# Attention with each query scaled and rotated two heads ahead

## The chip, the cores and the metric

The kernel runs on one core of a Trainium2 chip. The metric is the device time of one execution in microseconds (us), as the median of several. A core has engines with queues of their own, which wait for one another through semaphores: TensorE (PE, matmuls and transposes), VectorE (DVE), ScalarE (ACT), GpSimd (POOL) and SyncE (SP, which issues the DMAs).

## What is computed

The program is two layers of a model on 512 tokens of width 1024: a layer with gated linear attention and an MLP, and a hybrid layer that adds a gated delta rule and a sparse attention, with another MLP. The change touches the sparse attention of the second layer. For each of 8 query heads (2 key heads, 4 query heads to each, head size 128):

```
a_q = apply_partial_rope(rms_norm_2(a_q.reshape(B, S, ATT_HEADS, ATT_HEAD_DIM), q_norm_g), cos, sin)
...
s = jnp.einsum('bqcgd,bqncd->bqcgn', qg, k_g).astype(jnp.float32) * scale
s = jnp.where(valid[:, :, None, None, :], s, -jnp.inf)
p = jax.nn.softmax(s, axis=-1).astype(v_g.dtype)
o = jnp.einsum('bqcgn,bqncd->bqcgd', p, v_g)
```

The keys that a query may see (`valid`) are chosen once for all heads by an indexer, ahead of this stage. `apply_partial_rope` rotates the first 32 of the 128 dimensions by an angle that depends on the token.

## The kernel before

The kernel runs stage by stage, with a fence between the larger ones. The stage here is `pe_att`, `act_att`, `dve_att` and `pool_att`, one function for each engine. It stands behind the input projections and the choice of keys, and ahead of the delta rule (`pe_gdn` and so on). All operands lie in SBUF. The queries of all heads are in `q_all`, the reciprocal root mean squares of them in `q_sq`.

The loop `att_steps` goes through the heads in an order in which key head `e` alternates: step i = 2j + e. Two steps stand in the body of a loop over j that runs three times, and the last two are written out behind it. The scores of all 512 queries against the keys are made in four causal blocks of 512, 256, 128 and 384 keys (`S_ORDER`). Work of a step, with the lines of before:

- **scaling** of a query (`queries`, L1421, VectorE): query by gain by reciprocal root mean square, into `aq[:, e]`. It signals `r_y`.
- **rotation**: a matmul with the swap matrix on TensorE (`pe_rope`, L1112, in two passes), at the same time the product with the cosines on GpSimd (`pool_rope`, L1117), then two ops on VectorE (`dve_rope`): product of the matmul's result with the sines (L1123), and the sum (L1126), which signals `rp_out`.
- **scores** (L1374, TensorE): four matmuls, each in two passes (x8 in the rows). VectorE adds the mask as it takes them out of PSUM (L1436), takes the row maxima (L1440) and scales them (L1444).
- **softmax**: exponentials and row sums on ScalarE (L1408), reciprocals (L1452) and scaling of the probabilities (L1456) on VectorE.
- **transposes** of the probabilities (L1388, ten on TensorE), their copies out of PSUM on ScalarE (L1413), and the **product with the values** (L1395, four matmuls in eight passes).
- **output** (`output`, L1429, VectorE): result by gate, into `o_att`.

There are two buffers `aq` and `ms` (scores and probabilities), one for each e, and one PSUM bank for the rotation matmul. In step i of before, VectorE scales and rotates the query of head i+1 first, then normalizes head i, masks head i+1 and ends with the output of head i. TensorE rotates and scores head i+1 first, then transposes and multiplies head i. The engines' orders are fixed by this text; there is no scheduler.

Of the kernel before, what the change touches and what calls it, by code (L numbers as in the profile page):

```python
# [101 lines left out]
def build(nc, t, out, const_square, const_wide, gb_rows):  # L102
    with ExitStack() as ctx:
# [37 lines left out]
        def take(*shape):  # L141

            n = int(np.prod(shape))
            v = arena[:, at[0]:at[0] + n]
            at[0] += n
            assert at[0] <= 22400, at[0]
            if len(shape) == 2:
                v = v.rearrange("p (a b) -> p a b", a=shape[0])
            if len(shape) == 3:
                v = v.rearrange("p (a b c) -> p a b c", a=shape[0], b=shape[1])  # L150
            return v
# [883 lines left out]
        ca, sa = take(SEQ), take(SEQ)  # L1035
# [9 lines left out]
        aq = take(2, SEQ)  # L1045
# [62 lines left out]
        def pe_rope(pe, c, src, swap):  # L1108

            if not (isinstance(c, int) and c == 0):  # L1110
                pe.wait_ge(s["rp_ss"], c)
            pe.matmul(b[5][:], swap[:], src, start=True, stop=True).then_inc(s["rp_ps"], 1)  # L1112
# [6 lines left out]
        def dve_rope(dve, c, src, sin):  # L1119
            if not (isinstance(c, int) and c == 0):  # L1120
                dve.wait_ge(s["rp_out"], c)
            dve.wait_ge(s["rp_ps"], c + 1)
            dve.tensor_tensor(rp_s, b[5][:], sin, ALU.mult).then_inc(s["rp_ss"], 1)  # L1123
            dve.wait_ge(s["rp_cc"], c + 1)
            dve.wait_ge(s["rp_ss"], c + 1)
            dve.tensor_tensor(src, rp_c, rp_s, ALU.add).then_inc(s["rp_out"], 1)  # L1126
# [225 lines left out]
        HPK = ATT_H // ATT_KV  # L1352
# [5 lines left out]
        def att_steps(eng, body):  # L1358

            with eng.Fori(0, HPK - 1) as j:  # L1360
                body(j, 0, True)
                body(j, 1, True)
            body(HPK - 1, 0, True)
            body(HPK - 1, 1, False)

        def pe_att(pe):
            def front(i, e):

                pe.wait_ge(s["r_y"], i + 3)
                pe_rope(pe, i + 7, aq[:, e], swap_a)  # L1370
                pe.wait_ge(s["rp_out"], i + 8)
                for q in S_ORDER:
                    bk, o = s_at[q]
                    last = pe.matmul(bk[:, o:o + P * (q + 1)], aq[:, e, q * P:(q + 1) * P], ak[:, e, 0:P * (q + 1)],  # L1374
                                     start=True, stop=True)
                    if q != 0:
                        last.then_inc(s["s_ps"], 1)

            def body(j, e, more):
                i = 2 * j + e  # L1380
                if more:
                    pe.wait_ge(s["ms_r"], TT * i + TT)
                    front(i + 1, 1 - e)
                pe.wait_ge(s["pn_r"], TT * i + TT)
                for k in K_ORDER:
                    bk, o = t_at[k]
                    for q in range(k, TT):
                        last = pe.transpose(bk[:, o + (q - k) * P:o + (q - k + 1) * P],  # L1388
                                            ms[e][:, off[q] + k * P:off[q] + (k + 1) * P], ident[:])
                    if k != 3:  # L1390
                        last.then_inc(s["pt_ps"], 1)
                pe.wait_ge(s["att_done"], i + 1)
                for n, k in enumerate(K_ORDER):
                    pe.wait_ge(s["pt_sb"], TT * i + n + 1)
                    last = pe.matmul(b[4][:, k * P:SEQ], v_key[e][:, k, :], p_t[:, koff[k]:koff[k] + SEQ - k * P],  # L1395
                                     start=(n == 0), stop=(n == TT - 1), skip_group_check=True)
                last.then_inc(s["pv_ps"], 1)

            front(0, 0)
            att_steps(pe, body)  # L1400

        def act_att(act):
            def body(j, e, more):
                i = 2 * j + e
                act.wait_ge(s["nms"], i + 1)
                for q in S_ORDER:
                    m = ms[e][:, off[q]:off[q] + P * (q + 1)]
                    act.activation(m, m, ACT.Exp, scale=P ** -0.5, bias=n_max[:, 4 * e + q:4 * e + q + 1],  # L1408
                                   accum_out=r_sum[:, q:q + 1]).then_inc(s["ex_a"], 1)
                for n, k in enumerate(K_ORDER):  # L1410
                    act.wait_ge(s["pt_ps"], (TT - 1) * i + (1, 2, 3, 3)[n])
                    bk, o = t_at[k]
                    act.copy(p_t[:, koff[k]:koff[k] + SEQ - k * P], bk[:, o:o + SEQ - k * P]).then_inc(s["pt_sb"], 1)  # L1413

            att_steps(act, body)

        def dve_att(dve):
            def queries(j, e):
                i, h = 2 * j + e, j + HPK * e
                dve.wait_ge(s["r_r"], h + 3)  # L1420
                dve.scalar_tensor_tensor(aq[:, e], q_all[:, bass.ds(h, 1)].rearrange("p a t -> p (a t)"),  # L1421
                                         gains[:, G_QN:G_QN + 1], q_sq[:, bass.ds(h, 1)].rearrange("p a t -> p (a t)"),
                                         ALU.mult, ALU.mult).then_inc(s["r_y"], 1)

            def output(j, e):
                i, h = 2 * j + e, j + HPK * e
                dve.wait_ge(s["pv_ps"], i + 1)
                o = o_att[:, bass.ds(h, 1)].rearrange("p a t -> p (a t)")
                dve.scalar_tensor_tensor(o, o, 1.0, b[4][:], ALU.add, ALU.mult).then_inc(s["att_done"], 1)  # L1429

            def scores(i, e):
                for n, q in enumerate(S_ORDER):
                    dve.wait_ge(s["s_ps"], (TT - 1) * i + (1, 2, 3, 3)[n])
                    w = P * (q + 1)
                    bk, o = s_at[q]
                    dve.scalar_tensor_tensor(ms[e][:, off[q]:off[q] + w], sel[:, off[q]:off[q] + w], BIG, bk[:, o:o + w],  # L1436
                                             ALU.mult, ALU.add).then_inc(s["ms_r"], 1)
                for n, q in enumerate(S_ORDER):
                    dve.wait_ge(s["ms_r"], TT * i + n + 1)
                    dve.tensor_reduce(n_max[:, 4 * e + q:4 * e + q + 1], ms[e][:, off[q]:off[q] + P * (q + 1)], AX.X, ALU.max,  # L1440
                                      negate=True).then_inc(s["nm_r"], 1)
                dve.wait_ge(s["nm_r"], TT * i + TT)
                nm = n_max[:, 4 * e:4 * e + 4]
                dve.tensor_scalar(nm, nm, P ** -0.5, None, ALU.mult).then_inc(s["nms"], 1)  # L1444

            def body(j, e, more):
                i = 2 * j + e
                if more:
                    queries(j + e, 1 - e)
                    dve_rope(dve, i + 8, aq[:, 1 - e], sa)  # L1450
                dve.wait_ge(s["ex_a"], TT * i + TT)
                dve.reciprocal(r_sum, r_sum).then_inc(s["rs_r"], 1)  # L1452
                dve.wait_ge(s["rs_r"], i + 1)
                for q in S_ORDER:
                    m = ms[e][:, off[q]:off[q] + P * (q + 1)]
                    dve.tensor_scalar(m, m, r_sum[:, q:q + 1], None, ALU.mult).then_inc(s["pn_r"], 1)  # L1456
                if more:
                    scores(i + 1, 1 - e)
                output(j, e)

            queries(0, 0)
            dve_rope(dve, 7, aq[:, 0], sa)
            scores(0, 0)
            att_steps(dve, body)

        def pool_att(pool):
# [684 lines left out]
        @block.tensor  # L2151
        def _(pe):
            pe_start(pe)
            pe_norm(pe)
            pe.wait_ge(s["memsets"], 3)
            fence(pe, 1)
            pe_gates(pe)
            pe_gla(pe)
            pe.wait_ge(s["gla_done"], GLA_H + 1)
            fence(pe, 2)  # L2160
            pe_wout(pe, N_WO0, 0, 2 * (GLA_H - 1))
            pe_mlp(pe, N_FF0, 0, KT)
            fence(pe, 3)
            pe_two_norms(pe)
            pe_in1(pe)
            pe_att(pe)
            fence(pe, 4)
            pe_gdn(pe)
            pe.wait_ge(s["gdn_done"], GDN_H + 1)
            fence(pe, 5)  # L2170
            pe_wout(pe, N_WO1, 1, GDN_H - 1)
            pe_mlp(pe, N_FF1, 1, 3 * KT)
            pe_out(pe, KT - 1)
# [83 lines left out]
```

## Time and profile before

| | us |
|---|---|
| median of 3 runs | 1844.41 (1842.42 to 1846.32) |
| profiled execution | 1836.11 |
| its span, from first to last record | 1834.5 |
| TensorE busy | 1693.3 (92%) |
| VectorE busy | 1014.1 (55%) |
| ScalarE busy | 715.4 (39%) |
| GpSimd busy | 247.9 (14%) |

All times in rows below are those of the profiled execution, counted from the start of its span. A row of the chain of waits is a piece of the path that ended last: when it began, how long it held the path, and which engine and line it was. The attention stage lies in it from 882.6 to 976.4 us.

### The profile page before, as it was taken

How to read it: one execution, taken by the hardware profiler on the slowest of the kernel's cores; microseconds unless marked ns; L12 is line 12 of the kernel's file. 1: busy time of each engine (PE TensorE's matmuls, PEld its weight loads, DVE VectorE, ACT ScalarE, POOL GpSimd, SP SyncE). 2: the span in 40 equal slices, each digit the busy share in tenths (PEclk: the TensorE clock that was granted, in tenths of full speed). 3: DMA queues.
4: the chain of work that ended last, by engine and by line, in shares of the span. 5: the costliest groups of instructions: out<-in, count | busy, mean ns of one | idle time of the engine just before them, and what ended most of it. 6: DMA issues, size and time to landing. Idle time of an engine off the chain costs nothing.

```text
span 1834.5 us, 25379 instructions
## 1 busy us (share of the span) xinstructions
PE 1693.3 (92%) x9258; PEld 1327.9 (72%) x9258; DVE 1014.1 (55%) x1511; ACT 715.4 (39%) x1106; POOL 247.9 (14%) x216
## 2 busy tenths in 40 slices
PE   6899968999999978899668999999998899999999
PEld 3788856888888855567336777777776678888887
DVE  5455545444454455478676566766575544444443
ACT  6344433323132334224434455555454342323232
POOL 0134440000000030234110222211122000000000
PEclk8999979999999998999899999999999999999999
DMA  4222202233333332223002222222121233333333
GB/s 133 69 59 69 70 12 81 81 104 91 103 92 93 101 99 58 56 68 85 23 0 58 70 54 63 58 63 62 50 58 36 60 89 99 96 93 97 96 95 101
DMA packets 258153, 135.01 MB, mean 74 GB/s; under 512 B 10700, under 2 KB 254941, under 8 KB 258069
## 3 DMA queue, kind: packets, MB, share of 16 engines
q1 hardware_dynamic: 258068, 133.84, 26.2%
q8 instruction: 59, 0.97, 0.2%
q14 instruction: 26, 0.21, 0.0%
HBM read 131.64 MB, written 2.18 MB: 73 GB/s over the span
## 4 chain that ended last, share of the span: by engine, by line
PE 69%; DVE 12%; issue 10%; POOL 4%; ACT 3%; DVEq 1%; DMA 0%; POOLq 0%; ACTq 0%; PEldq 0%; SPq 0%; PEld 0%
PE bank L231 15%; PE bank L233 15%; PE bank L232 15%; PE bank L1616 4%; PE bank L490 4%; PE bank L492 3%; PE bank L491 3%; DVE arena L1316 1%; POOL arena L781 1%; PE bank L1374 1%; POOL arena L798 1%; PE bank L1112 1%; PE bank L1395 1%; DVE arena L1312 1%; DVE w_lo L215 1%
## 5 line engine op out<-in xcount | busy, mean ns | idle before, releaser
L215 DVE TENSOR_TENSOR w_lo<-raw,w_hi 128x1024 fp32r<-128x1024 f32 x218 | 280.9, 1289 | 103.8 <-ACT w_hi L211 100.8
L211 ACT CAST w_hi<-raw 128x1024 fp32r<-128x1024 f32 x234 | 245.0, 1047 | 229.2 <-PE bank L233 213.1
L231 PE MATMUL bank<-h_hi,w_hi 128*128 128x512 f32 x760 | 306.1, 403 | 24.7 <-DVE h_lo L993 10.2
L232 PE MATMUL bank<-h_lo,w_hi 128*128 128x512 f32 x760 | 298.8, 393 | 0.0
L233 PE MATMUL bank<-h_hi,w_lo 128*128 128x512 f32 x760 | 298.8, 393 | 0.0
L231 PE MATMUL bank<-m_hi,w_hi 128*128 128x512 f32 x608 | 239.2, 393 | 6.9 <-DVE w_lo L215 6.7
L233 PE MATMUL bank<-m_hi,w_lo 128*128 128x512 f32 x608 | 238.1, 392 | 0.0
L232 PE MATMUL bank<-m_lo,w_hi 128*128 128x512 f32 x608 | 237.8, 391 | 0.0
L490 PE MATMUL bank<-h_hi,w_hi 128*128 128x512 f32 x472 | 211.6, 448 | 0.0
L231 PEld LDWEIGHTS bank<-h_hi,w_hi 128*128 128x128 f32 x760 | 144.6, 190 | 70.7 <-issue 20.2
L492 PE MATMUL bank<-h_hi,w_lo 128*128 128x512 f32 x472 | 186.3, 395 | 0.0
L491 PE MATMUL bank<-h_lo,w_hi 128*128 128x512 f32 x472 | 185.8, 394 | 0.0
L232 PEld LDWEIGHTS bank<-h_lo,w_hi 128*128 128x128 f32 x760 | 144.9, 191 | 31.4 <-issue 2.5
L233 PEld LDWEIGHTS bank<-h_hi,w_lo 128*128 128x128 f32 x760 | 144.4, 190 | 30.7
L231 PEld LDWEIGHTS bank<-m_hi,w_hi 128*128 128x128 f32 x608 | 115.0, 189 | 34.1 <-issue 7.3
L233 PEld LDWEIGHTS bank<-m_hi,w_lo 128*128 128x128 f32 x608 | 114.8, 189 | 24.2
L232 PEld LDWEIGHTS bank<-m_lo,w_hi 128*128 128x128 f32 x608 | 114.9, 189 | 23.6
L929 DVE TENSOR_TENSOR arena<-bank,arena 128x512 f32<-128x512 f32 x64 | 44.3, 692 | 147.0 <-PE bank L233 147.0
L919 DVE TENSOR_TENSOR arena<-arena 128x512 f32<-128x512 f32 x64 | 44.3, 692 | 133.2 <-ACT arena L895 133.2
L490 PEld LDWEIGHTS bank<-h_hi,w_hi 128*128 128x128 f32 x472 | 89.5, 190 | 29.7 <-issue 13.1
L895 ACT ACTIVATE arena<-bank 128x512 f32<-128x512 f32 x64 | 38.5, 601 | 175.3 <-PE bank L233 175.3
L1616 PEld LDWEIGHTS bank<-arena 64*64 64x64 f32 x1984 | 74.6, 139 | 43.2 <-issue 35.8
(275 smaller groups left out, 2285.5 us busy)
## 6 DMA issues: line engine op xcount, KB each, us to landing
raw<-in_l_w_ff SPq DMA_DIRECT2D x64, 512.0 KB, 4.0
raw<-in_w_in SPq DMA_DIRECT2D x64, 512.0 KB, 3.8
raw<-in_w_mlp_up SPq DMA_DIRECT2D x32, 512.0 KB, 4.0
raw<-in_w_mlp_down SPq DMA_DIRECT2D x32, 512.0 KB, 3.9
raw<-in_l_w_in SPq DMA_DIRECT2D x24, 512.0 KB, 3.8
raw<-in_l_w_out SPq DMA_DIRECT2D x8, 512.0 KB, 3.7
arena<-gb_rows SPq DMA_DIRECT2D x16, 256.0 KB, 3.9
raw<-in_w_out SPq DMA_DIRECT2D x8, 512.0 KB, 3.8
```

The costliest lines, as they stand in the source:

```text
L211: act.copy(w_hi[q.par][:], raw[q.par][:]).then_inc(s["w_hi_ready"], 1)
L215: dve.tensor_tensor(w_lo[q.par][:], raw[q.par][:], w_hi[q.par][:].bitcast(F32), ALU.subtract).then_inc(s["w_ready"], 1)
L231: pe.matmul(g_bank[q.par][:], w_hi[q.par][:, k], hi[:, k], start=(k == 0), stop=False)
L232: pe.matmul(g_bank[q.par][:], w_hi[q.par][:, k], lo[:, k], start=False, stop=False)
L233: last = pe.matmul(g_bank[q.par][:], w_lo[q.par][:, k], hi[:, k], start=False, stop=(k == KT - 1))
L490: pe.matmul(g_bank[q.par][:], w_hi[q.par][:, k], hi[:, k], start=(k == 0), stop=False)
L491: pe.matmul(g_bank[q.par][:], w_hi[q.par][:, k], lo[:, k], start=False, stop=False)
L492: last = pe.matmul(g_bank[q.par][:], w_lo[q.par][:, k], hi[:, k], start=False, stop=(k == KT - 1))
L895: act.activation(rl[:, u % 2], g_bank[q.par][:], ACT.Relu).then_inc(s["rl"], 1)
L919: dve.tensor_tensor(sq[:, u % 2], rl[:, u % 2], rl[:, u % 2], ALU.mult).then_inc(s["sqr"], 1)
L929: dve.tensor_tensor(down[:, u % 2], g_bank[q.par][:], r_sqr, ALU.mult).then_inc(s["dn"], 1)
L1616: return pe.matmul(o, left, right, start=True, stop=True, skip_group_check=True)
```

## The change

The scaling and rotation of a query move from one head ahead to two heads ahead. The boolean `more` becomes a number `ahead` (2 in the loop, 1 and 0 in the last two steps). TensorE's `front` is split: the rotation matmul (`turn`) of head i+2 is issued behind the product with the values of head i, and the scores (`scores`) of head i+1 stay at the start of the step. On VectorE the scaling of head i+2 is issued behind the row maxima of head i+1, ahead of the output of head i, and the rotation's two ops behind that output. Ahead of the loop, head 1 is scaled and rotated beside the scores of head 0. ScalarE's and GpSimd's orders are as before.

```diff
             with eng.Fori(0, HPK - 1) as j:
-                body(j, 0, True)
-                body(j, 1, True)
-            body(HPK - 1, 0, True)
-            body(HPK - 1, 1, False)
+                body(j, 0, 2)
+                body(j, 1, 2)
+            body(HPK - 1, 0, 1)
+            body(HPK - 1, 1, 0)
 
         def pe_att(pe):
-            def front(i, e):
+            def turn(i, e):
 
                 pe.wait_ge(s["r_y"], i + 3)
                 pe_rope(pe, i + 7, aq[:, e], swap_a)
+
+            def scores(i, e):
                 pe.wait_ge(s["rp_out"], i + 8)
...
-                if more:
+                if ahead >= 1:
                     pe.wait_ge(s["ms_r"], TT * i + TT)
-                    front(i + 1, 1 - e)
+                    scores(i + 1, 1 - e)
                 pe.wait_ge(s["pn_r"], TT * i + TT)
...
                 last.then_inc(s["pv_ps"], 1)
-
-            front(0, 0)
+                if ahead >= 2:
+                    turn(i + 2, e)
+
+            turn(0, 0)
+            scores(0, 0)
+            turn(1, 1)
             att_steps(pe, body)
...
-            def body(j, e, more):
+            def body(j, e, ahead):
                 i = 2 * j + e
-                if more:
-                    queries(j + e, 1 - e)
-                    dve_rope(dve, i + 8, aq[:, 1 - e], sa)
                 dve.wait_ge(s["ex_a"], TT * i + TT)
...
-                if more:
+                if ahead >= 1:
                     scores(i + 1, 1 - e)
+                if ahead >= 2:
+                    queries(j + 1, e)
                 output(j, e)
+                if ahead >= 2:
+                    dve_rope(dve, i + 9, aq[:, e], sa)
 
             queries(0, 0)
             dve_rope(dve, 7, aq[:, 0], sa)
+            queries(0, 1)
             scores(0, 0)
+            dve_rope(dve, 8, aq[:, 1], sa)
             att_steps(dve, body)
```

On TensorE, the first step of the loop before. L1112 is the rotation matmul of the next head, L1374 its scores, L1388 the transposes and L1395 the product with the values of the head in hand:

```order
L1369 REGISTER_ALU
L1111 REGISTER_ALU
L1112 MATMUL bank<-arena,swap_a 128x512
L1371 REGISTER_ALU
L1374 MATMUL bank<-arena 128x512
L1374 MATMUL bank<-arena 128x256
L1374 MATMUL bank<-arena 128x128
L1374 MATMUL bank<-arena 128x384
L1388 MATMUL bank<-ident,arena 128x128 x10
```

The same step after the change, where the scores are L1376, the transposes L1390 and the product with the values L1397:

```order
L1376 MATMUL bank<-arena 128x384
L1390 MATMUL bank<-ident,arena 128x128 x10
L1394 REGISTER_ALU
L1396 REGISTER_ALU
L1397 MATMUL bank<-arena 128x512
L1396 REGISTER_ALU
L1397 MATMUL bank<-arena 128x256
L1396 REGISTER_ALU
L1397 MATMUL bank<-arena 128x128
L1397 MATMUL bank<-arena 128x384
L1369 REGISTER_ALU
L1112 MATMUL bank<-arena,swap_a 128x512
```

The rotation matmul has moved from the place directly ahead of the scores of its own head to behind the product with the values of the head two before it.

On VectorE, from the end of one step to the reciprocal of the next, before: L1444 ends the maxima, L1429 is the output, L1421 the scaling, L1123 and L1126 the rotation.

```order
L1444 TENSOR_SCALAR arena<-arena 128x4
L1429 ISA
L1429 SCALAR_TENSOR_TENSOR arena<-arena,bank 128x512
L1421 ISA
L1421 SCALAR_TENSOR_TENSOR arena<-q_all,gains,q_sq 128x512
L1122 REGISTER_ALU
```

After the change the maxima end with L1450, the scaling is L1427, the output L1435 and the reciprocal L1455:

```order
L1450 TENSOR_SCALAR arena<-arena 128x4
L1426 REGISTER_ALU
L1427 ISA
L1427 SCALAR_TENSOR_TENSOR arena<-q_all,gains,q_sq 128x512
L1435 ISA
L1435 SCALAR_TENSOR_TENSOR arena<-arena,bank 128x512
L1121 REGISTER_ALU
L1122 REGISTER_ALU
L1123 TENSOR_TENSOR arena<-bank,arena 128x512
L1126 TENSOR_TENSOR arena<-arena 128x512
L1455 RECIPROCAL arena<-arena 128x4
```

Scaling and output have changed places; the two ops of the rotation follow the output as before.

## Rows read from the trace of the kernel before

**Rows 1.** The page, its first line.

```profile
span 1834.5 us, 25379 instructions
```

**Rows 2.** Chain of waits, one head in mid-loop: start us, us, engine and line.

```profile
910.28 2.43 PE bank L1374 x8
912.71 1.09 PE bank L1388 x10
...
913.82 2.44 PE bank L1395 x8
...
916.40 0.06 DVE arena L1429
...
917.05 0.71 DVE arena L1421
...
917.88 1.14 PE bank L1112 x2
919.04 0.70 DVE arena L1123
...
919.84 0.70 DVE arena L1126
...
920.59 2.43 PE bank L1374 x8
```

**Rows 3.** Chain of waits, start of the stage.

```profile
886.22 4.65 PE bank L1374 x8
...
893.26 0.05 DVE arena L1444
...
893.60 0.76 DVE arena L1421
...
894.48 2.08 PE bank L1112 x2
...
898.13 4.33 PE bank L1374 x8
```

**Rows 4.** Timeline of VectorE: start, us, engine, line, op, out<-in, idle time before.

```profile
920.45 0.17 DVE L1452 RECIPROCAL arena<-arena 128x4 f32<-128x4 f32 x1
920.65 1.27 DVE L1456 TENSOR_SCALAR arena<-arena 128x512 f32<-128x512 f32 x4
921.84 1.01 DVE L1436 SCALAR_TENSOR_TENSOR arena<-arena,bank 128x512 f32<-128x512 f32 x2
...
923.72 1.66 DVE L1440 TENSOR_REDUCE arena<-arena 128x1 f32<-128x512 f32 x4
925.41 0.17 DVE L1444 TENSOR_SCALAR arena<-arena 128x4 f32<-128x4 f32 x1
```

**Rows 5.** Timeline of GpSimd in the same head as rows 2.

```profile
917.91 1.26 POOL L1117 TENSOR_TENSOR arena<-arena 128x512 f32<-128x512 f32 x1 [8.97 <-DVE arena L1421]
```

**Rows 6.** Chain of waits, last head to the next stage (L231).

```profile
961.71 2.44 PE bank L1374 x8
...
966.53 0.18 DVE arena L1444
...
966.74 2.30 ACT arena L1408 x8
...
970.60 2.39 PE bank L1388 x10
...
976.40 0.50 PE bank L231
```

**Rows 7.** Stretches: us, busy PE, PEld, DVE, ACT, POOL, granted clock, DMA share, GB/s.

```profile
898.00:902.00 4.00, 3.87 (x8) 2.36 (x9) 2.55 (x8) 0.00 (x0) 0.00 (x0) 0.50 0.00 0
902.00:904.00 2.00, 1.97 (x13) 1.43 (x12) 1.50 (x4) 1.06 (x4) 0.00 (x0) 0.99 0.00 0
910.00:920.00 10.00, 7.06 (x28) 4.01 (x28) 7.21 (x19) 3.70 (x12) 1.26 (x1) 1.00 0.00 0
971.00:973.00 2.00, 2.00 (x11) 2.00 (x10) 0.00 (x0) 0.86 (x2) 0.00 (x0) 0.50 0.00 0
```

More of the change, by code:

```diff
@@ L1397, in body @@
                 last.then_inc(s["pv_ps"], 1)
-            front(0, 0)
+                if ahead >= 2:
[3 more added lines that the diff above has]
+            turn(1, 1)
             att_steps(pe, body)
         def act_att(act):
-            def body(j, e, more):
+            def body(j, e, ahead):
                 i = 2 * j + e
@@ L1444, in scores, with body @@
                 dve.tensor_scalar(nm, nm, P ** -0.5, None, ALU.mult).then_inc(s["nms"], 1)
-            def body(j, e, more):
+            def body(j, e, ahead):
                 i = 2 * j + e
-                if more:
-                    queries(j + e, 1 - e)
-                    dve_rope(dve, i + 8, aq[:, 1 - e], sa)
                 dve.wait_ge(s["ex_a"], TT * i + TT)
```

## The prediction

> **What bounds the kernel now.** I read the page first, for the span [rows 1], and then the chain of waits through the attention stage, since only that stage is touched. The profiled execution took 1836.11 us around a span of 1834.5 us, so 1.6 us lie outside the span. The chain for one head in the middle of the loop [rows 2] is the base of everything below. TensorE computes the scores of the next head (2.43 us from 910.28), the ten transposes of the head in hand (1.09) and its product with the values (2.44), which ends at 916.26. Then nobody but VectorE has work: the output op (L1429) starts at 916.40, the scaling of the next query (L1421) at 917.05, TensorE rotates it from 917.88 (1.14), VectorE finishes the rotation with L1123 (919.04) and L1126 (919.84), and the next scores start at 920.59. So of each round 5.98 us are TensorE's big products, 1.62 us are output and scaling ahead of the rotation, and 2.71 us are the rotation itself. From 910.28 to the scores of the last head at 961.71 [rows 6] there are five rounds, (961.71 − 910.28) / 5 = 10.29 us each.
>
> Two other stretches differ. At the start [rows 3] the scores of head 0 take 4.65 us, the maxima end with L1444 at 893.26, and only then is head 1 scaled (893.60), rotated (894.48, 2.08 us) and multiplied (898.13). The matmuls there take about twice their later time (4.33 against 2.43, 2.08 against 1.14) because the granted clock was 0.50 in 898 to 902 (the 1.2 GHz level); it was 0.99 in 902 to 904 and 1.00 after [rows 7]. The round from 898.13 to 910.28 is thus 12.15 us. At the end [rows 6] nothing overlaps the last head, and from the scores at 961.71 to the next stage at 976.40 are 14.69 us.
>
> **The change, part by part.** I call the heads 0 to 7 in the order of the loop. Scaling and rotation of head i+2 now stand behind the row maxima of head i+1 and around the output of head i. Nothing is added or removed in count: eight scalings, eight rotations, and no DMA.
>
> *Middle rounds.* I lay VectorE out from the start of L1126 (919.84 is zero). As before [rows 4], the reciprocal starts at 0.61, the scaling of the probabilities at 0.81, masking at 2.00, the maxima at 3.88, and the small L1444 at 5.57. Now the scaling of the next query follows. The gap from L1444 to L1421 is 0.34 us at the start, with a loop branch in it [rows 3]; I take 0.30, so it runs from 5.87 to 6.62 (0.75 us). In the rows of before the rotation matmul starts 0.12 us behind the end of that op (917.76 to 917.88), so it could start at 6.74. TensorE itself has scores from 0.75 and the product with the values until 0.75 + 5.98 = 6.73. The two arrive together, which is the tight place of this change. Rotation at 6.75, L1123 at 6.75 + 1.16 = 7.91 (917.88 to 919.04), L1126 at + 0.80 = 8.71: that is the new round. The output op starts 0.14 us behind the product (6.87) and ends at 7.56, in the shadow of the rotation matmul; if that shadow were gone it would cost its 0.69 us. GpSimd's product (L1117, 1.26 us, 0.15 us behind the scaling [rows 5]) runs from 6.77 to 8.03, and L1126 needs it at 8.71. The exponentials (2.30 us [rows 6]) start 0.21 us behind L1444, end at 8.1, and the reciprocal wants them at 8.71 + 0.61. So a round goes from 10.29 to 8.71, saving 1.58; five of them save **7.9 us**. Bounds: if TensorE runs from one product into the next without a gap and VectorE's gap is 0.2, the round is 8.6 (saves 8.4); if the gap between L1444 and the scaling is twice the 0.34 of the row, it is 9.1 (saves 6.0).
>
> *Start.* The rotation matmul of head 1 follows the scores of head 0 directly (890.87, done at 892.95 even at 2.08 us). VectorE takes its result after L1444, a 0.17 us op [rows 4]: L1123 at about 893.26 + 0.21 = 893.47, L1126 at 894.27, scores of head 1 at 895.02 instead of 898.13. Saves **3.1 us**.
>
> *First round.* It was 12.15. Here the exponentials of head 0 are late: they can't start before 893.47 and end at 895.77, where in a middle round they are long done, so the reciprocal is at 895.8 and not at 894.9. If the clock is high, VectorE is the limit: scaling 896.0, masks 897.2, maxima 898.9, L1444 at 900.6, query scaled by 901.6, next scores 901.7 + 2.71 = 904.4, a round of 9.4. If it stays at 0.50 for the scores, as it did before, TensorE is: 4.33 + 3.55 + 0.05 + 2.71 = 10.65. I can't tell which, because TensorE now works without a break from 886.22 to near 892.9 but then waits about 2 us. I take 10.0: saves **2.1 us** (1.5 to 2.75).
>
> *End.* The last two heads keep their order; from the scores of head 7 to the next stage stays 14.69. In it the clock was at 0.50 in 971 to 973 [rows 7], and the transposes took 2.39 instead of 1.09. **0**, with 1.45 us to gain if that drop falls away. The branch of TensorE's loop now lies between a rotation and the scores behind it, under the 1.5 us of L1123 and L1126: 0.
>
> Sum: 3.1 + 2.1 + 7.9 = 13.1 us. Of the profiled 1836.11 us that leaves 1823.0. The median of the three runs shown is 8.3 us above the profiled execution, so I take the difference off it: 1844.41 − 13.1 = **1831.3 us**.
>
> **A rule weighed.** In the new order GpSimd's product lies beside the output op and L1123; before, it lay in an empty stretch of VectorE but for its very end. In the row it ran from 917.91 to 919.17, L1123 began at 919.04 inside it, and took its usual 0.70 [rows 2, 5]. The overlap is 0.13 us, too short to be proof. The Trainium skill, "SBUF — State Buffer", section "Who interferes with whom", says that a VectorE instruction with two SBUF inputs contends with a GpSimd instruction that reads SBUF, one fully blocking the other, and that one with at most one SBUF input does not. By that rule the output op and L1123, each with one operand from a PSUM bank, are free, and L1126, with two operands in SBUF, starts after the product. The sum would be the same 13.1 us; a reader who knows only that two engines share a port would subtract the 4.9 us of the second case below.
>
> **The rivals.**
> (1) *Forecast*, gain 11 to 15 us: chance 0.75.
> (2) *VectorE or GpSimd is late next.* If the output op had to wait for GpSimd's product (to 8.03), it would end at 8.72, L1126 would be at 9.52, and a round loses 0.81 us; six rounds lose 4.9. A gap of 0.7 us more ahead of the scaling would do the same. Gain 8.2: 1836.2 us. For it speaks that the query arrives within 0.1 us of when TensorE wants it; against it the L1123 row. Chance 0.10.
> (3) *The clock gives more.* TensorE was busy 7.06 of 10 us in 910 to 920 [rows 7] and would be busy 7.1 of 8.7. If the first round runs fast (0.6) and the drop at the end is gone (1.45), the gain is 15.2, 1829.2 us. If the runs behind the median, longer than the profiled one, had lost the clock for one head more, which the new order avoids, 6.3 us come on top (price below), 1823. Chance 0.09.
> (4) *It does nothing*: the rotation is still released by something behind the output, so that scaling and output merely swap. The round stays near 10.3 and only a part of the start is won. The order of instructions speaks against it. Within 0.2% of before: chance 0.02.
> (5) *Slower, by the clock.* The clock rose only after TensorE had worked unbroken from 898.13 to about 902. The new start breaks its work at 893 to 895, and if the level then stays at 1.2 GHz, each head costs 1.90 more for scores (4.33 against 2.43), 1.30 for transposes (2.39 against 1.09), 0.94 for the rotation and about 2.2 for the product with the values (an estimate: the same doubling, no row of it at that level): 6.3 us. From 13.1 / 6.3 = 2.1 heads on it decides; with four heads it is 12 us slower, 1856 us. Against it: every head now has 7 us of unbroken TensorE work, longer than the stretch that raised the clock. Chance 0.04.
>
> **How the numbers follow.** 0.2% is 3.7 us, about what a measurement of this kernel can tell from no change. (1), (2) and (3) are faster: 0.94. (4) is within: 0.02. (5) is slower: 0.04. The range runs from 1826, between the two figures of (3), to 1838, which is (2) with the 2 us by which the three runs lie about their median.
>
> **What would show it.** In the profile after: the scores of head 1 start about 8.8 us behind those of head 0 (11.9 before); rounds of 8.7 us between scores; the first one between 9.4 and 10.7; from the first scores to the next stage 77 us instead of 90.2; TensorE's idle time ahead of the rotation matmul nearly gone; the output op at its 0.69 us beside GpSimd's 1.27. I am wrong if the rotation matmul waits for the scaling for over 0.3 us in the middle rounds, if L1123 waits for the output op, or if the granted clock is 0.50 in any round but the first.

## The result, and the profile after

| | us |
|---|---|
| median before (4 runs) | 1844.59 (1842.42 to 1846.32) |
| median of the change (4 runs) | 1822.97 (1821.78 to 1824.64) |
| ratio of the runs | 0.9887, 95% interval 0.9873 to 0.9902 |
| profiled execution of the change | 1821.78, its span 1820.2 |

The change is faster by 21.6 us; the prediction was 13.1. The two profiled executions differ by 14.3 us in time and in span. So the profile moved about as forecast, and the median by half as much again as the profile.

The chain of waits of the changed kernel, at the start, in one head of mid-loop and at the end (scores are L1376 now, transposes L1390, product with the values L1397, the small op behind the maxima L1450):

```profile
span 1820.2 us, 25383 instructions
```

```profile
885.35 4.65 PE bank L1376 x8
...
892.38 0.04 DVE arena L1450
...
892.46 0.70 DVE arena L1123
...
894.00 4.11 PE bank L1376 x8
...
904.28 2.43 PE bank L1376 x8
...
912.86 2.43 PE bank L1376 x8
915.28 1.09 PE bank L1390 x10
...
916.40 2.43 PE bank L1397 x8
918.82 1.06 PE bank L1112 x2
...
919.91 0.70 DVE arena L1123
...
920.70 0.70 DVE arena L1126
...
921.45 2.43 PE bank L1376 x8
...
947.30 2.41 PE bank L1376 x8
...
956.16 2.39 PE bank L1390 x10
...
961.92 0.50 PE bank L231
```

Against [rows 2]: output and scaling are gone from the chain, and the rotation matmul follows the product with the values in the same instant (918.82). A middle round is 921.45 − 912.86 = 8.59 us, five of them (947.30 − 904.28) / 5 = 8.60; it was 10.29. Against [rows 3]: from the scores of head 0 to those of head 1 it is 8.65 us (11.91 before), and the first round is 10.28 (12.15). Against [rows 6]: the end is 14.62 (14.69). The stage, first scores to next stage, takes 76.6 us instead of 90.2. The last 0.7 of the 14.3 us had been gained ahead of it: the first scores start 0.87 us earlier than in the other execution, with nothing changed there.

VectorE and GpSimd in the timeline of the same head (start, us, engine, line, op, idle before):

```profile
917.68 0.17 DVE L1450 TENSOR_SCALAR arena<-arena 128x4 f32<-128x4 f32 x1
917.94 0.75 DVE L1427 SCALAR_TENSOR_TENSOR arena<-q_all,gains,q_sq 128x512 f32 x1
...
918.85 1.28 POOL L1117 TENSOR_TENSOR arena<-arena 128x512 f32<-128x512 f32 x1 [7.31 <-DVE arena L1427]
918.99 0.69 DVE L1435 SCALAR_TENSOR_TENSOR arena<-arena,bank 128x512 f32 x1 [0.30 <-PE bank L1397]
...
919.91 0.69 DVE L1123 TENSOR_TENSOR arena<-bank,arena 128x512 f32<-128x512 f32 x1 [0.23 <-PE bank L1112]
```

The scaling starts 0.26 us behind L1450 (0.30 was taken) and is done at 918.69, 0.13 us ahead of the 918.82 at which the chain turns to the rotation matmul. The margin is no larger than that: the load of the rotation's weights starts at 918.74, and the trace names the scaling as what released it. The output op keeps its 0.69 us beside GpSimd's 1.28 us, and L1123 waits for the matmul, not for the output.

### The profile page after: what moved, and what is told of

It reads as the page before. It is cut to its first block, busy times and chain, and to the rows that moved or that the text cites. A ratio compares the mean times of both kernels' runs of the same rounds, so it can differ in the third digit from the quotient of the medians.

```text
span 1820.2 us, 25383 instructions
## 1 busy us (share of the span) xinstructions
PE 1691.0 (93%) x9258; PEld 1328.1 (73%) x9258; DVE 1014.0 (56%) x1511; ACT 715.5 (39%) x1106; POOL 249.8 (14%) x216
## 4 chain that ended last, share of the span: by engine, by line
PE 69%; DVE 12%; issue 10%; POOL 4%; ACT 3%; DVEq 1%; DMA 0%; SPq 0%; POOLq 0%; ACTq 0%; PEldq 0%
PE bank L231 15%; PE bank L233 15%; PE bank L232 15%; PE bank L1625 4%; PE bank L490 4%; PE bank L492 3%; PE bank L491 3%; DVE arena L1316 1%; POOL arena L781 1%; PE bank L1376 1%; POOL arena L798 1%; DVE w_lo L215 1%; PE bank L1397 1%; DVE arena L1312 1%; PE bank L1112 1%
## 5 line engine op out<-in xcount | busy, mean ns | idle before, releaser
L231 PE MATMUL bank<-h_hi,w_hi 128*128 128x512 f32 x760 | 306.2, 403 | 25.1 <-DVE h_lo L993 10.2
L231 PE MATMUL bank<-m_hi,w_hi 128*128 128x512 f32 x608 | 239.2, 393 | 6.9 <-DVE w_lo L215 6.6
L231 PEld LDWEIGHTS bank<-h_hi,w_hi 128*128 128x128 f32 x760 | 144.5, 190 | 70.3 <-issue 19.7
L231 PEld LDWEIGHTS bank<-m_hi,w_hi 128*128 128x128 f32 x608 | 114.9, 189 | 34.2 <-issue 7.3
L490 PEld LDWEIGHTS bank<-h_hi,w_hi 128*128 128x128 f32 x472 | 89.5, 190 | 29.7 <-issue 13.1
```

Source lines behind the costliest of these rows:

```text
L231: pe.matmul(g_bank[q.par][:], w_hi[q.par][:, k], hi[:, k], start=(k == 0), stop=False)
L490: pe.matmul(g_bank[q.par][:], w_hi[q.par][:, k], hi[:, k], start=(k == 0), stop=False)
```

## The experiments

The question is where 7.3 us come from that no term of the sum has. The profiled execution of before was 8.3 us below the median that the prediction had (8.5 below that of the four runs), that of the change 1.2 us below its own. "This" below is the median of the kernel of the experiment, "before" that of the kernel before on the same chip.

### The kernel before, profiled once more

No edit.

> The kernel before, unchanged, profiled once more. The timed gain (21.6 us) is 7.3 us above what the two profiled executions differ by (14.3 us in both time and span), because the profiled execution of before was 8.3 us under the median. Clock theory: in most executions of before some rounds of the attention stage run partly at the low clock, since TensorE waits in two pieces of 1.6 us in each round; the stage from the first scores to the next stage is then about 97 to 99 us instead of 90.2, at 1840 to 1846 us in all, with granted clock below 1.00 in the middle rounds. Rival: the 8 us lie outside the stage (another chip, transfers); the stage is then 90.2 us again and some other stretch is longer.

Measured: the profiled execution took 1845.78 us, with these scores and last lines in the chain of waits:

```profile
888.98 4.65 PE bank L1374 x8
...
900.89 4.40 PE bank L1374 x8
...
913.10 4.63 PE bank L1374 x8
...
926.02 4.63 PE bank L1374 x8
...
939.02 4.11 PE bank L1374 x8
...
951.02 2.43 PE bank L1374 x8
...
971.58 2.44 PE bank L1374 x8
...
986.19 0.50 PE bank L231
```

and in its stretches (us, busy PE, PEld, DVE, ACT, POOL, granted clock, DMA share, GB/s):

```profile
910.00:913.00 3.00, 1.12 (x2) 0.30 (x2) 1.68 (x4) 0.18 (x2) 1.26 (x1) 0.79 0.00 0
913.00:917.00 4.00, 3.90 (x8) 2.39 (x9) 2.51 (x8) 0.00 (x0) 0.00 (x0) 0.50 0.00 0
...
948.00:958.00 10.00, 7.06 (x28) 4.01 (x28) 7.20 (x19) 3.39 (x12) 1.26 (x1) 1.00 0.00 0
```

In [rows 7] the first round was the only one at the low level. Here the clock falls in the middle rounds too. In 910 to 911 it is still 1.00, while the rotation matmul runs; in 912 to 913, in the wait behind it, it is 0.50 (0.79 over 910 to 913), and the scores that follow run at 1.2 GHz (0.50 in 913 to 917). The scores are slow in four rounds (those from 900.89, 913.10, 926.02 and 939.02), which take 12.2, 12.9, 13.0 and 12.0 us. The last two are 10.2 and 10.3, as in the first profile. The six rounds take 70.7 us against 63.6, and the stage 97.2 against 90.2: 7.0 of the 9.7 us between the two executions of one and the same kernel. The other 2.7 lie ahead of the stage, in work that is the same in all kernels here: the first scores start at 886.22 in the one profile and at 888.98 in the other. This profile is of one of the slowest of its ten executions, whose median is 1840.53 us.

What the others did is an estimate. In the ten profiles without extra matmuls ahead of the stage the first scores start between 885.35 and 889.74 us, and in all fourteen the rest behind the stage takes 856.8 to 859.9 us. With the 1.6 us outside the span, a stage of 90.2 us would give at most 889.7 + 90.2 + 859.9 + 1.6 = 1841.4 us. All four runs behind the median of 1844.59 are above that, and so are more than half of the 46 executions below.

Over 46 executions of the kernel before in all comparisons, the time went from 1834.72 to 1849.41 us and the mean granted clock of an execution from 0.967 to 0.956; their correlation is −0.95. This shows that time and clock go together, not in which stage. As a measure of such ratios: this run against before gave a ratio of 0.9981 (0.9962 to 0.9999) for two identical kernels, which is what a spread of 15 us does to a few runs.

### TensorE kept at work in the two waits, in the kernel before

```diff
-            def front(i, e):
+            def front(i, e, more=True):
+                if more:
+                    pe.matmul(b[0][:], ones[:], ca, start=True, stop=True)
                 pe.wait_ge(s["r_y"], i + 3)
                 pe_rope(pe, i + 7, aq[:, e], swap_a)
+                if more:
+                    pe.matmul(b[0][:], ones[:], ca, start=True, stop=True)
                 pe.wait_ge(s["rp_out"], i + 8)
...
-            front(0, 0)
+            front(0, 0, False)
```

> Before, with two matmuls of no use in each round of attention (ones by the cosine table into a scores bank that has been read), one in each of TensorE's two waits: ahead of the rotation matmul and behind it. Each lasts about 1.0 us and the waits 1.62 and 1.55 us, so in a run that keeps its clock they change nothing. Clock theory: median 6 to 9 us below before (1836 to 1838 us), granted clock 1.00 in every round but the first. Rival (the time lies elsewhere): the same as before within 2 us, or slower by what the fillers push in the slow first round (up to 1.5 us).

Measured: 1838.35 us (1836.36 to 1842.41, 7 runs), ratio 0.9969 (0.9953 to 0.9985). That is 5.9 us under before, but only 2.2 under the identical kernel of the run above. Against the median of all 28 executions of before on that chip (1843.5) it is 5.2 us. So the fillers help, by somewhat less than the 6 to 9 us expected, and by how much is uncertain. In its profile all middle rounds are 10.3 us, and the stage takes 89.1.

### The same, and at the edges of the stage too

To the fillers of the rounds come some at the edges: two matmuls ahead of the first rotation and one behind it, two more behind the maxima of head 0, and two ahead of the transposes of the last head.

> Before, with matmuls of no use in both waits of each round and at the edges (two ahead of the first rotation, two more ahead of the scores of head 1, two ahead of the last transposes). Clock theory: the rounds are 10.29 us with granted clock 1.00, the edges as fast as in the run of the change with them; the stage is then about 85 us (97 in the profile of before that lost the clock), the median 1832 to 1836 us, and the single runs lie within 4 to 5 us of each other instead of 13. The rest of the distance to the change with the same fillers, 12 to 14 us, is then what the order alone is worth. Rival: the median stays at 1840 or above with runs spread over 10 us, so that the spread does not come from TensorE's waits in this stage.

Measured: 1830.63 us (1829.96 to 1834.16, 6 runs) against 1843.88 (1834.82 to 1849.27), ratio 0.9933 (0.9912 to 0.9954). The spread is 4.2 us instead of 14.5. The scores in the chain and one stretch:

```profile
891.15 2.44 PE bank L1378 x8
...
899.90 2.43 PE bank L1378 x8
...
910.13 2.43 PE bank L1378 x8
...
961.55 2.44 PE bank L1378 x8
...
970.45 1.31 PE bank L1396 x10
```

```profile
900.00:910.00 10.00, 8.68 (x32) 4.67 (x32) 7.32 (x18) 3.71 (x12) 1.27 (x1) 1.00 0.00 0
```

Rounds of (961.55 − 910.13) / 5 = 10.28 us, the first one 10.23, and no low clock. The stage takes 84.0 us (the profile is of the longest of the six runs, 1834.16 us). Work of no use has made the kernel 13.2 us faster without touching its order, and put it below the 1832 to 1836 us expected. About 6 of these (90.2 − 84.0) are the edges and the first round, which ran at the low clock in the first profile too; about 7 are left for the middle rounds. So the waits of TensorE in this stage cost before twice: their length, and the clock behind them.

### The loop's part of the change, and the start alone

The loop alone scales head 1 behind the maxima of head 0:

```diff
             dve_rope(dve, 7, aq[:, 0], sa)
-            queries(0, 1)
             scores(0, 0)
+            queries(0, 1)
             dve_rope(dve, 8, aq[:, 1], sa)
```

> The change without its start: head 1 is scaled behind the maxima of head 0, as before; in the loop scaling stands ahead of the output as in the change. By the sum of terms the profiled execution is 8 to 9 us below that of before (rounds of 8.6 us instead of 10.29, five of them, and 1 us in the first round), the scores of head 1 about 11.9 us behind those of head 0. Clock theory: the timed gain against before is 15 to 17 us, since rounds of 8.6 us with one wait of 1.6 us keep the clock. Rival: 8 to 9 us timed as well.

Measured: 1827.71 us (1826.63 to 1829.72, 4 runs), ratio 0.9903 (0.9882 to 0.9924), 16.5 us under before. Rounds of 8.6 us, all with scores of 2.43 from the second on.

The start alone puts the output back ahead of the scaling:

```diff
-                if ahead >= 2:
-                    queries(j + 1, e)
                 output(j, e)
+                if ahead >= 2:
+                    queries(j + 1, e)
```

> The start of the change alone: head 1 is scaled and rotated beside the scores of head 0, but in the loop the output op stands ahead of the scaling, as before. By the sum of terms a gain of 3.1 us at the start and up to 2 us in the first round, rounds of 10.29 us after that: 3 to 5 us. Clock theory: rounds of 10.29 us with two waits lose the clock in most executions, so the timed gain is as small as the 3 to 5 us, and the profile shows low clock in middle rounds if its phase is unlucky.

Measured: 1837.31 us (1834.74 to 1839.83, 6 runs), ratio 0.996 (0.994 to 0.9981), 6.9 us under before. Its profile shows the low clock in middle rounds again:

```profile
897.95 3.90 PE bank L1376 x8
...
909.86 4.64 PE bank L1376 x8
...
922.73 4.04 PE bank L1376 x8
...
934.59 2.43 PE bank L1376 x8
```

The parts add up to 23.4 us against 21.6 for the whole, within their intervals. The start gives 6.9 us, more than the 3 to 5 expected and more than the 3.5 that its own profile has as terms (3.26 to the scores of head 1, 0.24 in the first round); the loop gives 16.5 where the rows of the profiles hold 9 to 10 (five times 1.69, and 12.15 − 10.69 = 1.5 in its first round). What both give beyond their rows fits the clock that the longer rounds lose, 7 us in the second profile of before.

### The change, profiled once more, and with its one wait filled

> The changed kernel, unchanged, profiled once more on another chip. Clock theory (a round with one wait of 1.6 us in 8.6 us keeps the high clock whatever the moment at which it starts, a round with two waits in 10.3 us does not): rounds of 8.58 us with granted clock 1.00 from the second on, as in the first profile, and single runs within 3 to 4 us of each other where those of before lie over 13 us; 19 to 23 us under before. Rival (the first profile of the change was lucky as well): a profile with 4.6 us scores in some middle rounds and runs spread as widely as those of before.

Measured: 1825.07 us (1824.75 to 1827.05, 4 runs) against 1841.38, ratio 0.9916 (0.9887 to 0.9945). Its middle rounds are 8.61 us at 2.43 us scores. The 16.3 us are less than the 19 to 23 expected, on a chip where before was 3 us faster.

```diff
                 if ahead >= 2:
                     turn(i + 2, e)
+                    pe.wait_ge(s["ms_r"], TT * i + 2 * TT)
+                    pe.matmul(b[0][:], ones[:], ca, start=True, stop=True)
```

> The change with one matmul of no use in each round, in the one wait that is left to TensorE (1.55 us behind the rotation). Clock theory: the middle rounds of the change keep the clock anyway, so this is the same within 1.5 us. Rival: the change loses the clock in some executions too, and this is 2 us or more faster.

Measured: 1824.90 us (1823.27 to 1829.26, 6 runs), ratio 0.9903 (0.9881 to 0.9926): the same as the change. The two are compared through their ratios to before, 0.9903 against 0.9887 and 0.9916 for the change, since the change alone was not run on this chip. To fill the one wait of 1.55 us in a round of 8.6 gains nothing that these runs can tell.

### The change with the edges filled

> The change with seven matmuls of no use (ones by the cosine table into a scores bank that has been read) where TensorE waits at the edges of the stage: two ahead of the first rotation, one behind it, two ahead of the scores of head 1, two ahead of the transposes of the last head. If waits at the edges are what drops the clock there: scores of head 0 in 2.4 instead of 4.65 us, of head 1 in 2.4 instead of 4.1, last transposes 1.1 instead of 2.4, and 2.2 + about 1 (VectorE is the limit of the first round) + 1.45 = 4 to 5 us less than the change. Rival: the clock follows something that a few matmuls don't settle, and the fillers cost up to 2 us where they run late at the low clock: the same as the change, or 1 to 2 us slower.

Measured: 1820.86 us (1817.93 to 1821.98, 4 runs), ratio 0.9886 (0.9856 to 0.9915), 4.2 us under the change on the same chip. The chain:

```profile
889.47 2.44 PE bank L1380 x8
...
905.27 4.04 PE bank L1380 x8
...
949.90 2.41 PE bank L1380 x8
...
958.77 1.31 PE bank L1397 x10
```

Scores of head 0, those of head 1 (2.43 us at 895.92) and the last transposes are fast. But the scores of head 2 (905.27) now run at the low level. TensorE's timeline shows two waits ahead of them:

```profile
902.56 1.12 PE L1112 MATMUL bank<-arena,swap_a 128*128 128x512 f32 x2 [0.44 <-DVE arena L1439]
...
905.27 4.04 PE L1380 MATMUL bank<-arena 128*128 128x512 f32 x8 [1.58 <-DVE arena L1126]
```

With fast matmuls at the start VectorE is the later one: the scaling of head 2 (L1439 here) comes 0.44 us after TensorE could use it, and behind the rotation come the usual 1.58 us. The granted clock was 1.00 in 902 to 904 and 0.50 from 905.2 to 908. It is the pattern of the kernel before, two waits around the rotation, in a kernel whose other rounds have one. It costs 1.6 us. Between this kernel and the filled kernel before, 12 to 14 us had been expected; the two stages take 73.95 and 83.95 us, 10.0 apart, and this slow head is one part of what is missing.

### The rotation still earlier

```diff
                 i = 2 * j + e
+                if ahead >= 2:
+                    queries(j + 1, e)
                 dve.wait_ge(s["ex_a"], TT * i + TT)
...
-                if ahead >= 2:
-                    queries(j + 1, e)
-                output(j, e)
                 if ahead >= 2:
                     dve_rope(dve, i + 9, aq[:, e], sa)
+                output(j, e)
```

On TensorE the rotation matmul of head i+2 stands behind the scores of head i+1.

> The change carried on: in the loop the query of head i+2 is scaled at the start of step i, its rotation matmul stands behind the scores of head i+1, and VectorE's two rotation ops stand behind the maxima of head i+1, ahead of the output of head i. The 1.55 us of VectorE between rotation matmul and scores leave TensorE's path. TensorE's own work per round is then 2.43 + 0.97 + 1.09 + 2.44 = 6.9 us, VectorE's ops add up to 7.7 to 7.9 us, so VectorE should be the bound: rounds of 7.8 us instead of 8.58 in five of them, 3 to 5 us less than the change. Rival: the scaling ahead of the reciprocal, with GpSimd's product beside the scaling of the probabilities, delays the chain maxima, exponentials, probabilities, and the round stays at 8.5 us or more: no gain.

Measured: 1823.21 us (1822.05 to 1826.78, 4 runs), ratio 0.991 (0.988 to 0.994), 1.9 us under the change on the same chip, with runs that overlap. Rounds of 8.60 us: the rival was right. The timeline shows why:

```profile
904.83 2.37 DVE L1461 TENSOR_SCALAR arena<-arena 128x512 f32<-128x512 f32 x4
904.86 0.51 PEld L1112 LDWEIGHTS bank<-arena,swap_a 128*128 128x128 f32 x2
904.87 1.26 POOL L1117 TENSOR_TENSOR arena<-arena 128x512 f32<-128x512 f32 x1 [8.16 <-DVE arena L1427]
```

The scaling of the probabilities takes 1.27 us where no product runs beside it (in this profile at 947.46, for the head before the last); beside GpSimd's product it takes 2.37, the longest of its single ops 1.58, and the transposes wait for it.

With the edges filled too:

> The rotation earlier as in the run before this one, together with the seven matmuls of no use at the edges. If both effects are real and apart from each other, the gains add up: 7 to 10 us under the change. If the fillers' effect is on the clock alone, the scores of heads 0 and 1 and the last transposes show 2.4, 2.4 and 1.1 us here too.

Measured: 1822.35 us (1820.49 to 1823.41, 4 runs), 2.7 us under the change. The edges are fast (scores of head 0 in 2.44, last transposes in 1.31 us), the rounds stay at 8.6. The expected 7 to 10 us under the change did not come. In the profile the stage is 71.6 us, 5.0 shorter than the 76.6 of the change, but the rest behind it takes 859.9 us instead of 858.3.

### The product beside the masking

The edit, against the kernel of the rotation still earlier:

```diff
-                if ahead >= 2:
-                    queries(j + 1, e)
                 dve.wait_ge(s["ex_a"], TT * i + TT)
...
+                if ahead >= 2:
+                    queries(j + 1, e)
                 if ahead >= 1:
                     scores(i + 1, 1 - e)
```

> As the run with the earlier rotation, but the query of head i+2 is scaled behind the scaling of the probabilities and ahead of the masking, so that GpSimd's product (1.26 us) lies beside the masking (one SBUF and one PSUM operand) and not beside the scaling of the probabilities. Port theory: in that run the scaling of the probabilities took 2.37 us instead of 1.27 because its first op waited for GpSimd's product; here it takes 1.27 again, and the round falls from 8.6 to 7.6 to 7.9 us, VectorE's own work: 4 to 5 us less than that run, 1817 to 1819 us. Rival: VectorE's chain of dependent ops is the limit in itself (8.6 us by the sum of ops and gaps): rounds of 8.5 us with the scaling at 1.27 us.

Measured: 1821.82 us (1817.91 to 1825.59, 6 runs) against 1843.88, ratio 0.9885 (0.9862 to 0.9908). The timeline of one round:

```profile
912.10 1.27 DVE L1459 TENSOR_SCALAR arena<-arena 128x512 f32<-128x512 f32 x4
...
913.95 1.68 DVE L1442 SCALAR_TENSOR_TENSOR arena<-arena,bank 128x512 f32<-128x512 f32 x4
...
914.19 1.27 POOL L1117 TENSOR_TENSOR arena<-arena 128x512 f32<-128x512 f32 x1 [6.60 <-DVE arena L1427]
```

The scaling is back at 1.27 us, the masking takes its 1.68 us beside the product (1.67 without it in the run of the rotation still earlier), and a round is 7.9 us (scores at 903.08 and 934.71, four rounds). Scaling, masking, maxima and the exponentials between them now make up the chain; TensorE's rotation is off it. The expected 1817 to 1819 us were missed: the stage is 72.3 us, 3.7 shorter than with the rotation still earlier, but the medians, taken on two chips, are 1.4 apart, and single runs spread over 7.7 us.

> The same with the seven matmuls of no use at the edges of the stage. If the clock's gain at the edges (2.2 us for the scores of head 0, 1.3 for the last transposes) adds to the shorter rounds: 3 to 4 us below the run without them, 1813 to 1816 us, below all others.

Measured: 1818.86 us (1813.11 to 1822.19, 6 runs), ratio 0.9869 (0.9843 to 0.9894). That is 3.0 us below the run without the fillers, as expected, but not in the expected 1813 to 1816. It has the lowest median here, 6 us under the change with its wait filled on the same chip (1824.90); with runs of 1813 to 1816 and of 1822 it falls into two groups, at mean clocks of 0.971 to 0.972 and 0.964 to 0.966. Where the second group loses the clock is not shown: the one profile is of the first.

## Why the prediction was wrong, point by point

**What bounds the kernel, and the chain.** Right for the execution in the profile, but not for the slower ones. The rows of the first round showed what a low clock costs here; I took it for a matter of the start.

**Middle rounds.** Forecast 8.71 and a saving of 7.9 us for five; in the profile 8.60 and 8.4. The tight place held: the scaling is ready 0.13 us before TensorE turns to the rotation.

**Start, first round, end.** Forecast 3.1, 2.1 and 0; in the profile 3.26, 1.87 and 0.07. The sum of 13.1 stands against 13.6 in the stage. The structure of the change was costed to within half a microsecond, and none of the three signs of being wrong appeared: they all looked at the profile after, and the error lay in the executions of before that have no profile.

**The step that failed** is the one from the sum to the median: "The median of the three runs shown is 8.3 us above the profiled execution, so I take the difference off it." That treats the 8.3 us as something constant beside the stage. Most of it was in the stage, on the path that the change shortens. In the second profile of before, four of six rounds ran at 12 to 13 us instead of one, because TensorE waited in two pieces around a short matmul and the clock fell behind them: 7.0 us more in the stage. The change takes away one of the two waits, keeps the clock in its middle rounds, and so gains about that as well: 13.6 + 7 = 20.6 of the 21.6 measured. That the unprofiled executions behind the median lost their time in the same rounds is an estimate, by the bound of 1841.4 us above; the fillers bear it out in size (5.2 to 5.9 us in the rounds, about 7 with the edges filled too), less well the 2.2 us to the ten further executions of the identical kernel. The 1.0 us left over is within what the stretch ahead of the stage varies by.

**The rivals.** The third had the mechanism in its second half ("had lost the clock for one head more, which the new order avoids") and even the figure, 1823. The figure is in part luck: 2.05 us of it (a fast first round, 0.6, and fast last transposes, 1.45) did not come, since in the profile after the scores of head 1 take 4.11 and the last transposes 2.39 us. One slow head was priced at 6.3 us and the case at a chance of 0.09. Measured, a round that loses the clock costs 1.7 to 2.7 us (12.0 to 13.0 against 10.3), since only the scores and a part of the transposes are slow, and there are three such rounds more, not one. The evidence for a higher chance was in sight: a profiled execution 6 us below the fastest of three runs that lie within 4 us of each other. The range, from 1826, ended between the two figures of that rival, where nothing was likely to fall.

The second rival (GpSimd's product holds the output op) did not happen, by the rows at 918.85 and 918.99. The fifth (slower by the clock) neither: the granted clock is 1.00 in every stretch from 898 to 949.

**The rule weighed.** It held for the output op and L1123. I cited it short: the same section of the Trainium skill's "SBUF — State Buffer" excepts VectorE's 2-port performance modes and names `tensor_scalar` among the ops that can enter them. The run with the still earlier rotation agrees: a `tensor_scalar` with one SBUF tensor as input takes 1.27 us alone and 2.37 beside GpSimd. Which mode the op was in no run here shows.

## What to carry to other kernels

Before a sum is made from a profile, ask which execution it is: if it lies outside the timed runs, the missing time is part of the question, and the mean granted clock of each run shows whether TensorE's clock differs with it. A wait of TensorE has two prices, its length and the clock of what follows; the second differs from execution to execution and a single lucky profile hides it, and a few matmuls of no use in the wait give a measure of it. When an op is moved, look at what it comes to lie beside: the scaling of a query starts GpSimd's product, which cost nothing beside the output op and 1.1 us a round beside the probabilities' scaling.

## What was not expected of the hardware

Two waits of 1.6 us with a 1.1 us matmul between them lose the clock in some rounds and not in others of the same execution (scores of 4.63 us at 926.02 and of 2.43 us at 951.02). One wait of 1.55 us in a round of 8.6 us lost it in no middle round of three profiles (the change twice, and the loop's part alone). Even 0.44 us ahead of the rotation matmul and 1.58 behind it were followed by the low clock once (905.27 in the change with its edges filled). Two identical kernels gave medians of 1840.53 and 1844.21 us on one chip.
